# A streaming encoder step on one core: the weight split moved ahead of the sample-state updates, and prevT stored half by half

## What is computed

```python
proj = h @ w_in                       # z, x, B, C (and dt, earlier)
xbc_act = silu(causal 4-tap conv of the x, B, C columns)
# per group g of 8, 4 heads j each, p = 64 rows, n = 128 states
...
s_new  = s * dec[..., None, None] + chunk_state      # state of each stream
y_off  = einsum('bclgn,bcgjpn,bclgj->bclgjp', Cc, prev, exp(a_cs))
y      = y_diag + y_off
```

## Time and profile before

| | |
|---|---|
| median of 3 runs | 1962.87 us (1961.29 to 1965.03) |
| profiled execution | 1962.87 us, of which 1960.8 us are the span |
| TensorE busy | 1880.2 us, 96% of the span |
| DVE busy | 1278.9 us, 65% |
| ACT busy | 796.2 us, 41% |
| POOL busy | 300.6 us, 15% |
| mean granted clock of TensorE | 0.981 |

### The profile page before, as it was taken

How to read it: one execution, slowest core, us unless ns; L and a number is a source line. 1 busy time by engine, 2 the same in 40 slices (tenths; PEclk the granted TensorE clock), 3 DMA queues, 4 the chain that set the end, 5 groups by cost and what they waited for, 6 DMA issues and landing times.

```text
span 1960.8 us, 35226 instructions
## 1 busy us (share of the span) xinstructions
PE 1880.2 (96%) x13063; PEld 1760.4 (90%) x13063; DVE 1278.9 (65%) x2367; ACT 796.2 (41%) x1417; POOL 300.6 (15%) x353
## 2 busy tenths in 40 slices
PE   7899897899999999999999999999799999999998
PEld 7777465599999999998999999999699999999998
DVE  4388575435867677545778888878554685858654
ACT  4222473224434343333554455554333443434332
POOL 0001451011000000021343423333102000000001
PEclk9999699999999999998999999999899999999999
DMA  7532102422232323222244443345233222222321
GB/s 164 111 70 52 61 1 77 106 55 78 79 92 65 98 60 108 71 76 56 92 130 127 139 138 100 118 128 169 92 105 104 68 80 78 81 86 71 92 76 54
DMA packets 311565, 176.81 MB, mean 90 GB/s; under 512 B 39888, under 2 KB 305040, under 8 KB 310416
## 3 DMA queue, kind: packets, MB, share of 16 engines
q1 hardware_dynamic: 308752, 172.49, 31.0%
q10 hardware_dynamic: 2688, 2.62, 0.4%
HBM read 155.18 MB, written 19.72 MB: 89 GB/s over the span
## 4 chain that ended last, share of the span: by engine, by line
PE 72%; DVE 3%; issue 3%; ACT 2%; DVEq 0%; ACTq 0%
PE psum L1326 27%; PE psum L204 24%; PE psum L1354 14%; PE psum L583 1%; PE psum L559 1%; DVE conv_out L702 1%; PE psum L548 1%; PE psum L587 1%; PE psum L536 1%; ACT HH L1435 0%; PE psum L611 0%; PE psum L529 0%; PE psum L570 0%; DVE HL L1443 0%; PE psum L602 0%
## 5 line engine op out<-in xcount | busy, mean ns | idle before, releaser
L204 PE MATMUL psum<-b2H,WH 128*128 128x320 f32 x912 | 219.3, 322 | 13.1 <-DVE b2L L1137 12.2
L204 PE MATMUL psum<-b2H,WL 128*128 128x320 f32 x912 | 209.5, 311 | 0.0
L204 PE MATMUL psum<-b2L,WH 128*128 128x320 f32 x912 | 209.5, 311 | 0.0
L1326 PE MATMUL psum<-b2H,HT 128*128 128x320 f32 x816 | 186.5, 310 | 1.1 <-DVE xT L423 1.1
L1326 PE MATMUL psum<-b2L,HT 128*128 128x320 f32 x816 | 186.1, 309 | 0.0
L194 ACT ACTIVATE WH<-W 128x1024 fp32r<-128x1024 f32 x90 | 95.0, 1055 | 213.4 <-PE psum L204 187.2
L204 PEld LDWEIGHTS psum<-b2H,WH 128*128 128x128 f32 x912 | 151.1, 191 | 27.7 <-issue 26.5
L1354 PE MATMUL psum<-HH,HT 128*128 128x320 f32 x544 | 167.5, 308 | 1.5 <-DVE HL L1443 1.5
L1354 PE MATMUL psum<-HL,HT 128*128 128x320 f32 x544 | 167.9, 309 | 0.0
L198 DVE TENSOR_TENSOR WL<-W,WH 128x1024 fp32r<-128x1024 f32 x90 | 137.1, 1523 | 40.9 <-ACT WH L194 39.9
L204 PEld LDWEIGHTS psum<-b2L,WH 128*128 128x128 f32 x912 | 154.6, 190 | 0.0
(11 more groups left out here) (393 smaller groups left out, 4412.5 us busy)
## 6 DMA issues: line engine op xcount, KB each, us to landing
W<-ssm_w_in SPq DMA_DIRECT2D x98, 256.0 KB, 3.1
RW<-mlp_w_up SPq DMA_DIRECT2D x64, 256.0 KB, 3.0
RWx<-mlp_w_up SPq DMA_DIRECT2D x64, 256.0 KB, 3.1
RW<-mlp_w_down SPq DMA_DIRECT2D x64, 256.0 KB, 3.0
RWx<-mlp_w_down SPq DMA_DIRECT2D x64, 256.0 KB, 3.2
bc<-scratch_acs SPq DMA_DIRECT2D x8, 1280.0 KB, 7.4
W<-attn_w_in SPq DMA_DIRECT2D x32, 256.0 KB, 3.6
prev<-state_ssm SPq DMA_DIRECT2D x16, 512.0 KB, 5.4
```

The costliest lines, as they stand in the source:

```text
L204: last = pe.matmul(psum[0:m, 2 * b.slot + h, 0:TH], w[:, b.slot, k, 0:m], r[:, k, h * TH:(h + 1) * TH], start=(n == 0 and i == 0), stop=(n ...
L1326: last = pe.matmul(psum[:, i // 2 * 2 + h, 0:TH], w[:, k], x, start=(kx == 0 and c == 0), stop=(kx == 7 and c == 2))
```

## The change

Two things. In `conv_evac` the split of the slab comes straight behind the read-out of the block; `sample_states(u, 1)` follows it and no longer stands between the two. And `prevT` is stored with the half outermost, so that `copy_prev` writes one contiguous run of 1024 a row, and each product of `pe_read_prev` reads two runs of 128, one from each half.

```diff
--- before.py
+++ after.py
@@ -461,7 +461,7 @@
     Bc = sc("Bc", [P, T]); Cc = sc("Cc", [P, T]); xs = sc("xs", [P, 2, T]); C2 = sc("C2", [P, T])
     Btok = sc("Btok", [P, T]); cbm = sc("cbm", [P, T])
     xdt = sc("xdt", [P, 2, T]); xddt = sc("xddt", [P, 2, T])
-    ST = sc("ST", [P, 4, 2 * P]); prevT = sc("prevT", [P, DB, 2, P])
+    ST = sc("ST", [P, 4, 2 * P]); prevT = sc("prevT", [P, 2, DB, P])
     assert s2[0] <= b2_at
     stf = at("stf", [P, 2, P], F32, sq_at + 5120)
     y_in = at("y_in", [P, 2, T], F32, S0)
@@ -567,7 +567,7 @@
         for half in range(2):
             for i in range(4):
                 r = slice(32 * i, 32 * i + 32)
-                last = pe.matmul(psum[r, 5, 256:512], CE[:, half, r], prevT[:, 2 * i + half].rearrange("p a n -> p (a n)"),
+                last = pe.matmul(psum[r, 5, 256:512], CE[:, half, r], prevT[:, 0:2, 2 * i + half],
                                  start=(half == 0), stop=(half == 1))
         last.then_inc(tPV, 1)
 
@@ -672,7 +672,7 @@
         last.then_inc(acm, 1)
 
 
-    def conv_evac(dve, g, j, then=None):
+    def conv_evac(dve, g, j):
 
         b, m, s = Block(B_SSM + j, 3 * g), 4 * g + j, j % 2
         dve.wait_ge(mm_done, b.n + 1)
@@ -684,8 +684,6 @@
         dve.tensor_tensor(raw[:, s, 3 + SEQ:NR].rearrange("p (b i) -> p b i", b=DB)[:, :, 3:],
                           o[:, 1, SEQ - TH:].rearrange("p (b i) -> p b i", b=DB),
                           RS[:, SEQ:T].rearrange("p (b i) -> p b i", b=DB), ALU.mult).then_inc(out_free, 1)
-        if then:
-            then()
         split_lo(dve, Block(b.c + 2, b.v))
 
     def conv_taps(dve, g, j):
@@ -802,7 +800,9 @@
         if L:
             sample_states(dve, u, 0)
         conv_taps(dve, g, 0)
-        conv_evac(dve, g, 1, (lambda: sample_states(dve, u, 1)) if L else None)
+        conv_evac(dve, g, 1)
+        if L:
+            sample_states(dve, u, 1)
         conv_taps(dve, g, 1)
         if L:
             y_sums(dve, u, 0, g)
@@ -880,7 +880,7 @@
     def copy_prev(act, u, p):
         act.wait_ge(tPV, 3 * u + p + 1)
         wait(act, tY, 2 * u)
-        act.activation(prevT[:, :, p], bank(6, 1024, 2).rearrange("p (b n) -> p b n", b=DB), ACT.Copy).then_inc(pvc, 1)
+        act.activation(prevT[:, p].rearrange("p b n -> p (b n)"), bank(6, 1024, 2), ACT.Copy).then_inc(pvc, 1)
 
     def copy_read_rows(act, u):
         act.wait_ge(tPV, 3 * u + 3)
```

## The result

The changed kernel takes 1992.18 us (median of four runs, 1989.91 to 1995.55), the one before 1962.53 us beside it: the ratio is 1.0151, with a 95% interval of 1.0133 to 1.0169. It is slower by 29.7 us; 34.4 had been forecast. The profiled execution took 1994.71 us, of which 1992.7 are the span, 31.9 us more than the span of before.

A forecast was written before the change was run, and what follows sets the result against it. TensorE, busy for 96% of the span, was taken to bound the kernel. The sum was 1962.9 + 20.0 (waits) + 14.4 (clock) + 0 (layout) = 1997.3 us, range 1983 and a little under it to 2012.

The forecast's parts named there:

- The moved split: Second layer's state-space mixer: late updates make TensorE wait before L570 in seven groups, paid in full, 20.0 us.
- The clock: TensorE's clock falls to 0.50 behind six of the seven new waits, 2.4 us lost each, 14.4 us.
- the low stretch: Time TensorE runs at clock 0.50 behind a new wait: 5.3 us taken, 45% of it lost.
- the stretch behind 2.31 us: Earlier TensorE gap elsewhere in the kernel before, followed by clock 0.50 for 10.3 us; used to size the clock loss.
- The layout: prevT stored contiguously: no gain for ACT's copy, no cost for TensorE's read L570; 0 us, read bounds -8 and +8.
- Without clock loss: Rival: the seven TensorE waits cost 20.0 us but the clock stays up; 1982.9 us, chance 0.16.
- The long low stretch: Rival: every new TensorE wait is followed by the longest slow clock, 32.5 us in all; 2015 us, chance 0.09.
- the wait at the end of the stage: Rival: TensorE's 12.19 us wait for DVE's b2L at 1384.16 vanishes, giving part back; 1985 us, chance 0.04.
- the dearer read: Rival: two runs make TensorE's L570 cost twice as much, +8 us; 2005 us, chance 0.03.
- not slower: Rival: WH is there when DVE arrives, so the move costs nothing; at best 1962.4 us, chance 0.04.
- The likeliest case: The forecast itself: TensorE's new waits plus lost clock in the mixer stage, 1997 us, chance 0.64.

The follow-up runs named there:

- WH earlier: Changed kernel with ACT's split_hi for the slab of block 3 moved ahead of its silu of block 0: 1966.18 us, ratio 1.0020.
- the two partial orders: Changed kernel with four, or six, of the eight state updates ahead of the split and the others behind: 1976.5 us (1.0078) and 1971.87 us (1.0048).
- the wait filled: Changed kernel with 18 unused products on TensorE in front of its wait for the updates, in seven groups: 1983.48 us, ratio 1.0104.
- the layout alone: Kernel before with only the new prevT layout, DVE's old order kept: 1963.07 us, ratio 1.0004.

## Why the prediction was right

**The moved split.** Forecast 20.0 us in seven waits of 2.1, 2.5 and five of 3.1 us; the profile has 20.3 us in seven of 2.17 to 3.14. The step that WL can't start before WH, and that the updates go from DVE's waiting time to TensorE's path, is what "WH earlier" and the two partial orders showed. DVE's idle time was forecast at 2.2 us and is 2.18. The hand-over from DVE to L570 took 0.15 us where 0.05 was taken. That the wait is paid in full, and that the later taps, `y_sums`, SP and POOL add nothing to it, held as well: with the wait filled, the time is what the waits alone give, within 0.4 us.

**The clock.** Six of seven waits were forecast to lose it and six did in the profiled execution. The term was 14.4 us and is 11.6, what is left of the 31.9 us beside the waits; by the medians it is 9.4. What was mis-sized is the low stretch: 5.3 us forecast, between the means with and without the stretch behind 2.31 us; the six had a mean of 4.2 us. The mean without it, 4.5 us, was the better guide. The forecast was 34.4 us against 29.7 for the medians, and nearly all of the difference lies in this term. That just six of seven lost the clock is in part luck: nothing in the prediction says which wait would keep it, and the runs don't show it either. The clock also reached L570 itself, which was to stay at 1.00 us a group: its records go up to 636 ns in the changed kernel and to 635 ns with the old layout and the moved split, against 404 before, so that is the clock and not the layout.

**The layout.** 0 forecast; 0 measured for the copy and for the read, and nothing in the time of the layout alone.

**The rivals.** Without clock loss, 1982.9 us: that is what the filled wait showed, at 1983.48, and not what the change does. The long low stretch, the wait at the end of the stage that would give 12.2 us back (it stayed at 12.2), and the dearer read fell. In "not slower", WH had to land 3.0 us sooner, by 1272.45. "WH earlier" moved it by 3.3 us against L684, and the kernel is still at 1.0020. The condition was incomplete: DVE can't start the split before it has read block 1 out, which it had at 1273.25, and 1273.25 + 3.34 is 0.8 us past the start of L570. These 0.8 us a group are what stayed.

**The likeliest case's own range**, 1989 to 2005, held.

## What to carry to other kernels

Before moving an instruction ahead in a hand-written order, look at what its operand waits for: here the split had 0.04 us to spare, and work that seemed to be in its way was filling a wait. The engine that loses time by it (DVE, a third of its time free) isn't the one that pays. Where TensorE is full, price a new wait as its length plus the clock that may be lost behind it (here 0, 1.6 or 2.7 us), and ask first whether the producer (here ACT, idle for 7 to 9 us) can be made earlier.

## What the runs showed of the hardware

The length of a wait alone doesn't tell whether the clock falls. In the changed kernel the clock stayed at 1.00 behind one wait of 3.12 us and fell behind one of 2.17. With four updates ahead of the split, waits of 2.1 us kept it five times in five, with the same products around them as in the changed kernel, whereas in the kernel before the gap of 2.31 us, with a run of small products behind it, lost it for 10.3 us. These are counts of one profiled execution of each kernel. The Trainium skill (TensorE: Matmul & The Clock Gate, section "HAM oscillation — how this bites in real kernels") describes a loop in which waits of some 3 to 5 us lose the clock in every pass. No wait here is longer than 3.14 us; the clock was lost in six passes of seven with waits of 2.2 to 3.1 us, and in none of seven with waits of 2.1 us or less. A low stretch can begin while TensorE still waits, as at 1298.20, or once the products behind the wait already run, as behind 1235.53. And 18 products more in each of the seven groups made the kernel 9 us faster: the updates came as late as before, and the clock of the stage went from 0.97 to 1.00.
